# Projections of three tiles in three passes over w_main instead of four, with a weight ring of four chunks

## The chip, the cores and the metric

The kernel runs on one core of one Trainium2 chip. Its engines each run their own instruction stream and wait for each other by semaphores: TensorE (PE, matmuls, with weight loads listed as PEld), VectorE (DVE), ScalarE (ACT), GpSimd (POOL) and SyncE (SP), the last of which only issues DMAs here. The metric is the time of one execution on the device in microseconds; lower is better.

## The reference

One step of a one-layer streaming trunk in float32, for 1040 prompt rows (16 meta rows and 1024) and 32 sample rows that have 1040 cached rows before them. Per row it normalises x, projects it, runs two kinds of attention of 8 heads each, gates and merges them, and adds a product-key mixture: 128 experts per row (8 heads, 16 each) out of 16384, picked as the top 16 of the 256 sums of two top-16 lists.

```python
n = rms_norm(x, norm_mix)
fq, fk, fv, ff, sq, sk, sv, ga, gb = split(n @ w_in)      # 3*512 | 8 | 3*512 | 2*1024 columns
o_fox = fox_attention(fq, c[:, past:], fk_all, fv_all, c, q_pos, k_pos)
o_sb = stick_breaking_attention(sq, sk_all, sv_all, q_pos, k_pos)
y = (sigmoid(ga) * (o_fox @ w_o_fox) + sigmoid(gb) * (o_sb @ w_o_sb)) @ w_out
h = x + y
xt = rms_norm(h, norm_ffn)
act = gelu(einsum('thkd,td->thk', expert_u[eidx], xt))
out = h + einsum('thk,thkd->td', softmax(sc) * act, expert_v[eidx])
```

## The kernel before

The 1072 rows are nine tiles of 128 (tile 8, called SAMPLES, has 32 sample rows and the 16 meta rows). `WAVES` makes five waves of them: tiles 0 and 1, 2 and 3, 4 and 5, 6 and 7, and tile 8. Every wave g passes through project(g), attend(g) and merge(g). All five engines are written out in full by hand, in program order; there is no scheduler, and order between engines is by semaphores alone.

- **project(g)** (PE line 927, ACT 1186, DVE 1534, SP 603). `NEW` names the tiles that are projected in front of wave g: 0, 1 and SAMPLES for wave 0, then two each, and none for wave 4. `w_main` (all of w_in but the forget columns, 1024 x 5120) is read once per project call in ten columns of 512, each in two halves of 512 rows: twenty chunks of 1 MB. A chunk goes into the ring `wring` of `NW` = 3 buffers, which the merge's chunks (`w_stream`, 16 per wave) share. PE multiplies each half column with every tile's turned x (`xt`, for the third tile `xt_s`) into that tile's bank (`column_bank`, six: four of `pb` and two halves of `pv`), ACT copies it out to `stage` and stores it, q and k columns (`QK`) are also turned on PE. Before the first column PE waits for `xg_ready`: DVE multiplies the turned x by norm_mix once x_t is there. `forget()` on PE is the small product for the forget columns.
- **attend(g)**: 32 units (16 in wave 4), each a head, a tile and a kind. The keys and values of a pair of heads are loaded by SP (`load_pair`, line 516), from DRAM where the projection stored them. The first pair of waves 1 to 3 is issued inside project(g), at c == 7.
- **merge(g)**: products with w_o, gates, w_out, the residual, the norm, the expert queries, the picking of experts (`pick_halves`, `pick_experts` on DVE, the last of which raises `named`).
- **Expert work of the tiles of wave g - 1** runs beside the stages of wave g. POOL gathers for each of 128 slots a row of expert_u and expert_v for each of 128 rows (1 MB) into one of ten buffers `uv`. A lot is four slots: DVE makes four dots (line 1346), ACT the gelu, and each slot's sum is made on DVE (line 1369) or on PE (`background`, line 777). `Plan` deals the 64 lots of two tiles over the steps of the wave in proportion to `SHARE`; `ON_VECTOR` says how many of a lot's four sums DVE makes beside a step of that kind: four in projections, y and h, two in most of the merge, none while experts are picked, and in attention three in two lots (the default).

The lots of wave 1, 2 and 3 each: 13 in the projection, 26 in attention, 15 in the merge to the queries, 10 in the picking.

On SP everything is in one queue: an issue that has to wait holds all behind it. The arena (`carve`, lines 320 to 391) is one buffer of SBUF whose parts are used by several stages in turn.

## Time and profile before

| | us |
|---|---|
| median of three runs | 4275.64 |
| lowest, highest | 4275.32, 4285.22 |
| the profiled execution, its own time | 4279.13 |
| span of the profile | 4277.3 |
| TensorE, VectorE, ScalarE, GpSimd busy | 3242.6, 2864.9, 1216.8, 1389.5 |
| moved by DMA | 1388.17 MB, mean 325 GB/s |
| wave 0: projection, attention | 25 to 257, 257 to 377 |
| wave 1: projection, attention, merge | 601 to 832, 832 to 1129, 1129 to 1489 |
| wave 2: the same | 1491 to 1732, 1732 to 2053, 2053 to 2411 |
| wave 3: the same | 2413 to 2656, 2656 to 3028, 3028 to 3380 |
| wave 4: attention, merge; then the rest of the experts | 3395 to 3662, 3662 to 3930; to 4277 |

Busy time is that of one engine's instructions, a sum over stages with different limits. In a view of stretches, a row gives the stretch, its length, then the busy time and the number of instructions of PE, PEld, DVE, ACT and POOL, the granted clock of TensorE as a share of full speed, the busy share of the DMA engines and GB/s. In a timeline a row gives start, length, engine, line, operation, output and inputs by name, count, and in brackets the idle time before it and what ended it.

### The profile page before, as it was taken

How to read it: one execution, taken by the hardware profiler on the slowest of the kernel's cores; microseconds unless marked ns; L12 is line 12 of the kernel's file. 1: busy time of each engine (PE TensorE's matmuls, PEld its weight loads, DVE VectorE, ACT ScalarE, POOL GpSimd, SP SyncE). 2: the span in 40 equal slices, each digit the busy share in tenths (PEclk: the TensorE clock that was granted, in tenths of full speed). 3: DMA queues.
4: the chain of work that ended last, by engine and by line, in shares of the span. 5: the costliest groups of instructions: out<-in, count | busy, mean ns of one | idle time of the engine just before them, and what ended most of it. 6: DMA issues, size and time to landing. Idle time of an engine off the chain costs nothing.

```text
span 4277.3 us, 32195 instructions
## 1 busy us (share of the span) xinstructions
PE 3242.6 (76%) x9738; PEld 1679.2 (39%) x9738; DVE 2864.9 (67%) x5568; ACT 1216.8 (28%) x2591; POOL 1389.5 (32%) x1086
## 2 busy tenths in 40 slices
PE   8989838588868595798876785899876677868665
PEld 3345623244435242455453332555453233334222
DVE  2012477587678975688579775788679766557865
ACT  1132112255311121566111121666211245111110
POOL 0000013243433333343333232334333233434553
PEclk9966969687879798788888897888888777888787
DMA  4413439899999889799999798787998788999997
GB/s 138 134 53 120 141 139 415 335 380 400 391 370 386 322 328 414 279 383 374 390 392 360 278 400 345 298 348 307 384 391 328 277 316 324 408 420 385 385 420 321
DMA packets 306602, 1388.17 MB, mean 325 GB/s; under 512 B 36384, under 2 KB 96960, under 8 KB 159968
## 3 DMA queue, kind: packets, MB, share of 16 engines
q0 software_dynamic: 154464, 1116.02, 64.7%
q1 hardware_dynamic: 121056, 243.75, 15.9%
q10 hardware_dynamic: 30912, 26.35, 1.9%
q8 instruction: 80, 1.31, 0.1%
q14 instruction: 90, 0.74, 0.0%
HBM read 1350.49 MB, written 35.10 MB: 324 GB/s over the span
## 4 chain that ended last, share of the span: by engine, by line
PE 35%; DVE 28%; DMA 18%; ACT 7%; issue 6%; SPq 5%; POOL 1%; ACTq 0%; DVEq 0%; POOLq 0%
DVE uv L1346 11%; PE pb L946 9%; DMA uv<-expert_uv,rows_u 8%; PE pv L777 7%; SPq L526 5%; DMA arena<-w_main 5%; PE pb L887 3%; PE pb L860 3%; PE pb L730 3%; PE pb L759 2%; PE pb L835 2%; DVE held L1369 2%; DMA arena<-w_stream 2%; PE pv L946 2%; DVE arena L1407 1%
## 5 line engine op out<-in xcount | busy, mean ns | idle before, releaser
L680 POOL DMA_INDIRECT uv<-expert_uv,rows_u x1024 | 1334.8, 1304 | 2250.8 <-PE pv L777 1168.8
L777 PE MATMUL pv<-uv,diag 128*128 128x512 f32 x2316 | 1244.7, 694 | 377.4 <-ACT diag L1083 336.9
L1346 DVE CUSTOM_DVE_ANT_0 uv<-uv,nr 128x1024 f32<-128x1024 f32 x1056 | 1241.5, 1220 | 204.8 <-DMA uv<-expert_uv,rows_u 171.0
L777 PEld LDWEIGHTS pv<-uv,diag 128*128 128x128 f32 x2316 | 504.0, 226 | 1024.7 <-issue 982.4
L946 PE MATMUL pb<-arena 128*128 128x512 f32 x1280 | 620.9, 643 | 163.2 <-DMA arena<-w_main 163.1
L1369 DVE SCALAR_TENSOR_TENSOR held<-uv,wgt,held 128x1024 f32<-128x1024 f32 x477 | 613.0, 1285 | 16.9 <-DVE wgt L1357 0.3
L1090 ACT ACTIVATE gel<-dots 128x4 f32<-128x4 f32 x264 | 54.2, 205 | 1792.2 <-DVE dots L1346 1712.5
L946 PEld LDWEIGHTS pb<-arena 128*128 128x128 f32 x1280 | 258.9, 207 | 497.0 <-issue 316.9
L730 PE MATMUL pb<-arena 64*128 64x512 f32 (+6 forms) x544 | 281.2, 635 | 125.2 <-DVE arena L1328 43.0
L759 PE MATMUL pb<-arena 128*128 128x64 f32 (+3 forms) x1728 | 256.2, 297 | 40.3 <-ACT o L1072 40.3
L759 PEld LDWEIGHTS pb<-arena 128*128 128x128 f32 (+3 forms) x1728 | 237.1, 202 | 106.6 <-issue 68.5
L887 PE MATMUL pb<-arena 128*128 128x256 f32 (+1 forms) x1280 | 265.7, 367 | 4.5 <-ACT arena L1156 4.5
L887 PEld LDWEIGHTS pb<-arena 128*128 128x128 f32 x1280 | 230.6, 196 | 46.1 <-issue 12.4
L1357 DVE TENSOR_TENSOR wgt<-gel,gw 128x4 f32<-128x4 f32 x256 | 41.7, 163 | 282.2 <-ACT gel L1090 281.7
L1083 ACT ACTIVATE diag<-ident,wgt 128x128 f32<-128x128 f32 x579 | 194.1, 391 | 85.7 <-PE pv L777 59.3
L1336 DVE SCALAR_TENSOR_TENSOR arena<-arena 128x144 f32<-128x144 f32 (+4 forms) x72 | 59.8, 830 | 211.8 <-ACT arena L1037 207.5
L730 PEld LDWEIGHTS pb<-arena 64*128 64x128 f32 (+1 forms) x544 | 104.1, 223 | 244.6 <-issue 138.6
L701 POOL DMA_DIRECT2D held<-scratch_h x9 | 5.4, 601 | 562.0 <-DVEq L1467 561.7
L747 PE MATMUL pb<-ident,arena 128*128 128x128 f32 (+3 forms) x864 | 144.4, 304 | 44.2 <-ACT arena L1061 43.6
L1090 ACT ACT_TABLE_LOAD x130 | 166.8, 1283 | 7.4 <-ACT arena L1230 5.3
L835 PE MATMUL pb<-arena 128*128 128x512 f32 (+1 forms) x288 | 135.1, 627 | 27.1 <-DMA arena<-w_stream 25.8
L1061 ACT ACTIVATE arena<-pb 128x512 f32<-128x512 f32 (+2 forms) x224 | 94.5, 452 | 191.0 <-PE pb L747 189.0
(147 smaller groups left out, 2670.5 us busy)
## 6 DMA issues: line engine op xcount, KB each, us to landing
arena<-w_main SPq DMA_DIRECT2D x80, 1024.0 KB
arena<-w_stream SPq DMA_DIRECT2D x80, 1024.0 KB
uv<-expert_uv,rows_u POOLq DMA_INDIRECT x1024
arena<-x SPq DMA_DIRECT2D x16, 512.0 KB, 19.6
scratch_gates<-arena ACTq DMA_DIRECT2D x32, 256.0 KB, 11.3
arena<-scratch_gates SPq DMA_DIRECT2D x8, 1024.0 KB, 21.7
arena<-scratch_c_p SPq DMA_DIRECT2D x8, 520.0 KB
arena<-x_t SPq DMA_DIRECT2D x8, 512.0 KB
```

The source lines that it names most:

```text
L526: here = lambda dst, src: sp.dma_start(dst, src).then_inc(pair_in[b], 16)
L680: pool.indirect_dma_start(out=uv[k % NU][:].rearrange("p a n -> p (a n)"), out_offset=None, in_=io["expert_uv"][:, :], in_offset=bass.Indi ...
L730: mm = nc.tensor.matmul(pb[0:r, m % 3, 0:c1 - c0], qt[k][pair % 2][half, tj * P:tj * P + r], kt[k][pair % 2][half, c0:c1], start=True, sto ...
L759: mm = nc.tensor.matmul(po[0:r], probt[n % 2][0:w, slot, 0:r], vt[k][pair % 2][0:w, slot, hh * DH:(hh + 1) * DH], start=j == 0, stop=j == ...
L777: mm = nc.tensor.matmul(pv[:, c * BANK:(c + 1) * BANK], diag[n % ND][:], uv[k % NU][:, 1, c * BANK:(c + 1) * BANK], start=n == first, stop ...
L835: mm = nc.tensor.matmul(pb[0:r, ti * 2 + k, :], ot[:, k * 4 + f, ti * P:ti * P + r], wring[n % NW][:, f * BANK:(f + 1) * BANK], start=f == ...
L887: mm = nc.tensor.matmul(pb[:, 4 + h % 2, half * 2 * P:half * 2 * P + width], wring[n % NW][:, (f * 2 + half) * P:(f * 2 + half + 1) * P], ...
L946: mm = nc.tensor.matmul(column_bank(proj.slot(c, ti))[0:r], x_turned(ti, half * 4 + f, r), w[:, f, :], start=half == 0 and f == 0, stop=ha ...
L1083: nc.scalar.activation(diag[n % ND][:], ident[:], ACT.Copy, scale=wgt[b % 2][:, k % LOT:k % LOT + 1]).then_inc(diag_made, 1)
L1090: nc.scalar.activation(gel[b % 2][:], dots[b % 2][:], ACT.Gelu).then_inc(gelu, 1)
L1346: nc.vector.tensor_tensor_reduce(out=u, in0=u, in1=row[:], scale=1.0, scalar=0.0, op0=ALU.mult, op1=ALU.add, accum_out=dots[b % 2][:, k % ...
L1369: nc.vector.scalar_tensor_tensor(out=held[t % 2][:], in0=v, scalar=w[:, k % LOT:k % LOT + 1], in1=held[t % 2][:], op0=ALU.mult, op1=ALU.ad ...
```

## The change

`NEW` becomes (0, 1, SAMPLES), (2, 3, 4), (5, 6, 7) and nothing in front of waves 3 and 4. Passes over w_main go from four to three, and `NW` from 3 to 4.

- Three tiles take turns over four banks of `pb` (`bank`), in the order of their products, and PE waits until the copy of the product four before is made (`behind`). Slots of `stage` are six, by tile and parity of the column.
- The turned x of the third tile (`xt_third`) lies where picking works; SP loads it behind the first four weight chunks and, in waves 1 and 2, behind a wait for `named`.
- Room for the fourth ring buffer comes from moves in the arena: x of the merge (`xh`) now lies in the output rows `o`, so its load waits for `o_turned`; the picks' buffers, the queries and the row of norm_ffn (`g_row`) lie in the gates, so the load of norm_ffn waits for `merged` and stands in front of the first query chunk.
- `Plan` weighs a projection step by its tiles over two (1.4 becomes 2.1). The lots of waves 1 and 2 become 18 in the projection, 23 in attention, 14 and 9 in the merge; those of wave 3: 32 in attention, 20 in the merge to the queries, 12 in the picking.

```diff
-NW = 3
+NW = 4
-NEW = [(0, 1, SAMPLES), (2, 3), (4, 5), (6, 7), ()]
+NEW = [(0, 1, SAMPLES), (2, 3, 4), (5, 6, 7), (), ()]
...
+    def bank(self, g, c, ti):
+
+        return (c * len(NEW[g]) + ti) % 4
+
+    def behind(self, g, c, ti):
+
+        n = c * len(NEW[g]) + ti - 4
+        return self.staged[g, n // len(NEW[g]), n % len(NEW[g])] if n >= 0 else None
...
-            steps = [(("project", g, c), "project", SHARE["project"]) for c in range(COLS if NEW[g] else 0)]
+            steps = [(("project", g, c), "project", SHARE["project"] * len(NEW[g]) / 2) for c in range(COLS if NEW[g] else 0)]
...
-            count = self.tiles[g][0] * LOTS - first - (0 if NEW[g] else LEFT)
+            count = self.tiles[g][0] * LOTS - first - (0 if g < len(WAVES) - 1 else LEFT)
...
-        o = [[sb(f"o{k}{i}", [P, WID]) for i in range(2)] for k in range(KINDS)]
+        o_rows = [sb(f"o{i}", [P, KINDS, WID]) for i in range(2)]
+        o = [[o_rows[i][:, k, :] for i in range(2)] for k in range(KINDS)]
+        xh = [o_rows[i][:].rearrange("p k n -> p (k n)") for i in range(2)]
...
                     for c in range(NW):
                         load_half(g, c)
+                    if g:
+                        sp.wait_ge(named, plan.tiles[g][0])
+                    t = NEW[g][2]
+                    sp.dma_start(xt_third[:, :, 0:rows_of(t)],
+                                 io["x_t"][:, first_row(t):first_row(t) + rows_of(t)].rearrange("(k p) n -> p k n", p=P)).then_inc(xt_in, 16)
...
+                    sp.wait_ge(o_turned, tiles[-1] + 1)
                     for ti, t in enumerate(tiles):
                         r = query_rows(t)
                         sp.dma_start(xh[ti][0:r], io["x"][first_row(t):first_row(t) + r, :]).then_inc(x_in[ti], 16)
-                    sp.dma_start(g_row, io["norm_ffn"].partition_broadcast(P)).then_inc(g_in, 16)
                     for c in range(NW, 8 + NW):
+                        if c == NW + 4:
+                            sp.wait_ge(merged, 2 * (tiles[-1] + 1))
+                            sp.dma_start(g_row, io["norm_ffn"].partition_broadcast(P)).then_inc(g_in, 16)
                         load_chunk(g, c)
...
-                            if c >= 2 and half == 0:
-                                pe.wait_ge(staged, proj.staged[g, c - 2, ti])
+                            if half == 0 and proj.behind(g, c, ti):
+                                pe.wait_ge(staged, proj.behind(g, c, ti))
...
-                    pe.wait_ge(xg_ready, KD * (g + 1) + 1)
+                    pe.wait_ge(xg_ready, (KD + 1) * (g + 1))
```

Three places in the order of the built programs follow, since the sizes of the ring and of a pass move instructions that the diff doesn't name.

SP, the end of wave 1's projection, before: `w_main` is a weight chunk, `scratch_q_fox` to `out_sv_p` are the first attention pair (its loads of meta rows are left out), `scratch_c_p` the running forget sums.

```order
L561 DMA arena<-w_main 128x4x512 [waits proj_ready]
L526 DMA arena<-scratch_q_fox 128x256 [waits s_stored2,s_stored0,s_stored1,t_stored3,s_stored3,t_stored2,summed_up,t_stored1,t_stored0]
L526 DMA arena<-scratch_k_fox 128x528
L526 DMA arena<-out_fv_p 128x4x128
...
L526 DMA arena<-scratch_k_sb 128x528
L526 DMA arena<-out_sv_p 128x4x128
...
L561 DMA arena<-w_main 128x4x512 [waits chunk_used]
```

The same place after:

```order
L572 DMA arena<-w_main 128x4x512 [waits chunk_used]
L572 DMA arena<-w_main 128x4x512 [waits proj_ready]
L537 DMA arena<-scratch_q_fox 128x256 [waits s_stored1,s_stored3,s_stored4,s_stored0,s_stored2,t_stored3,s_stored5,t_stored2,summed_up,t_stored1,t_stored0]
L537 DMA arena<-scratch_k_fox 128x528
L537 DMA arena<-out_fv_p 128x4x128
```

The twentieth weight chunk stood behind the pair, and now stands ahead of it.

PE, wave 1, from the first chunk to the second of column 1, before: line 946 is a tile's product with a half column, line 962 the turning of a column, `chunk_in` a landed weight chunk, `staged` ACT's copy.

```order
L946 MATMUL pb<-arena 128x512 [waits chunk_in2]
L946 MATMUL pb<-arena 128x512 x7
L962 MATMUL pb<-ident,arena 128x128 [waits col_turned_out,normed]
L962 MATMUL pb<-ident,arena 128x128 x3
L946 MATMUL pb<-arena 128x512 [waits chunk_in0]
```

The same place after, with lines 965 and 981:

```order
L965 MATMUL pb<-arena 128x512 [waits chunk_in2]
L965 MATMUL pb<-arena 128x512 x3
L965 MATMUL pb<-arena 128x512 [waits staged]
L965 MATMUL pb<-arena 128x512 x3
L965 MATMUL pb<-arena 128x512 [waits staged]
L965 MATMUL pb<-arena 128x512 x3
L981 MATMUL pb<-ident,arena 128x128 [waits col_turned_out,normed]
L981 MATMUL pb<-ident,arena 128x128 x3
L965 MATMUL pb<-arena 128x512 [waits chunk_in3]
```

Column 1 waited for no copy before; now its second and third tile wait for the copies of column 0.

SP, from the last merge chunks of wave 2 to wave 3, before:

```order
L553 DMA arena<-w_stream 128x2048 [waits q_ready] x5
L582 DMA arena<-x_t 128x8x128 [waits q_ready,h_stored]
L582 DMA arena<-x_t 128x8x128
L588 DMA arena<-x 128x1024 [waits h_stored]
L588 DMA arena<-x 128x1024
L561 DMA arena<-w_main 128x4x512 [waits q_ready] x3
L561 DMA arena<-w_main 128x4x512 [waits chunk_used]
```

And after:

```order
L564 DMA arena<-w_stream 128x2048 [waits q_ready] x4
L537 DMA arena<-scratch_q_fox 128x256 [waits named,summed_up,q_out,h_stored]
L537 DMA arena<-scratch_k_fox 128x1040
L537 DMA arena<-out_fv_p 128x8x128
L537 DMA arena<-out_fv_p 16x128
L537 DMA arena<-scratch_q_sb 128x256
```

The loads of the projection are gone, and the first pair of wave 3 stands behind the naming of the experts.

## Rows read from the trace of the kernel before

**Rows 1.** The page: busy us by engine, share of the span, instructions.

```profile
PE 3242.6 (76%) x9738; PEld 1679.2 (39%) x9738; DVE 2864.9 (67%) x5568; ACT 1216.8 (28%) x2591; POOL 1389.5 (32%) x1086
```

**Rows 2.** Stretches: length, busy us by engine, clock, DMA share, GB/s; waves 0 to 3.

```profile
25.50:257.00 231.50, 220.98 (x535) 82.86 (x534) 24.25 (x58) 39.03 (x65) 0.00 (x0) 0.99 0.36 113
607.80:832.50 224.70, 163.53 (x359) 71.01 (x358) 142.24 (x207) 43.76 (x67) 69.79 (x50) 0.85 0.86 340
832.50:1129.00 296.50, 249.33 (x824) 133.40 (x824) 240.81 (x384) 170.69 (x365) 134.54 (x106) 0.82 0.95 382
1732.00:2053.00 321.00, 285.27 (x1032) 165.00 (x1032) 266.49 (x392) 200.75 (x412) 134.12 (x106) 0.82 0.91 363
2656.00:3028.00 372.00, 336.05 (x1273) 194.05 (x1274) 294.24 (x403) 230.62 (x429) 137.05 (x106) 0.82 0.84 326
3028.00:3250.00 222.00, 171.03 (x581) 107.57 (x582) 158.96 (x380) 29.53 (x63) 75.32 (x59) 0.87 0.94 378
3250.00:3385.00 135.00, 80.44 (x152) 32.89 (x151) 125.53 (x318) 20.70 (x53) 51.07 (x41) 0.80 0.82 320
```

**Rows 3.** The same view: program start, wave 1's projection, its end.

```profile
24.00:28.00 4.00, 4.00 (x20) 2.58 (x21) 0.00 (x0) 0.00 (x0) 0.00 (x0) 1.00 0.41 142
650.00:700.00 50.00, 43.21 (x106) 19.27 (x104) 43.12 (x62) 15.11 (x26) 23.02 (x16) 0.93 1.03 415
800.00:832.00 32.00, 10.04 (x16) 4.04 (x16) 3.40 (x4) 5.43 (x6) 1.75 (x1) 0.61 0.55 211
```

**Rows 4.** Timeline, TensorE, wave 1's projection: start, us, idle before and its releaser.

```profile
700.65 7.13 PE L946 MATMUL pb<-arena 128*128 128x512 f32 x16 [2.64 <-DMA arena<-w_main]
...
713.15 10.14 PE L946 MATMUL pb<-arena 128*128 128x512 f32 x16 [4.93 <-DMA arena<-w_main]
```

**Rows 5.** Timeline, the end of wave 1's projection: SP's issues and TensorE.

```profile
793.35 0.96 SPq L561 DMA_DIRECT2D arena<-w_main  x1
...
815.76 1.22 PE L946 MATMUL pb<-arena 128*128 128x512 f32 x1 [23.32 <-DMA arena<-w_main]
```

**Rows 6.** Timeline: last naming and next start, wave 3, then wave 4.

```profile
2405.60 1.23 DVE L1346 CUSTOM_DVE_ANT_0 uv<-uv,nr 128x1024 f32<-128x1024 f32 x1 [0.18 <-DVE gw L1464]
...
2656.79 2.07 PE L730 MATMUL pb<-arena 64*128 64x512 f32 x2 [7.87 <-DMA arena<-scratch_c_p]
...
3375.05 0.33 SPq L526 DMA_DIRECT2D arena<-scratch_q_fox  x1
...
3395.19 1.03 PE L730 MATMUL pb<-arena 64*32 64x512 f32 x1 [19.27 <-DMA arena<-scratch_c_s]
```

**Rows 7.** The page: background products, dots, sums (busy, mean ns), gathers, x loads.

```profile
L777 PE MATMUL pv<-uv,diag 128*128 128x512 f32 x2316 | 1244.7, 694 | 377.4 <-ACT diag L1083 336.9
L1346 DVE CUSTOM_DVE_ANT_0 uv<-uv,nr 128x1024 f32<-128x1024 f32 x1056 | 1241.5, 1220 | 204.8 <-DMA uv<-expert_uv,rows_u 171.0
L1369 DVE SCALAR_TENSOR_TENSOR held<-uv,wgt,held 128x1024 f32<-128x1024 f32 x477 | 613.0, 1285 | 16.9 <-DVE wgt L1357 0.3
q0 software_dynamic: 154464, 1116.02, 64.7%
arena<-x SPq DMA_DIRECT2D x16, 512.0 KB, 19.6
```

**Rows 8.** Timeline at the program's start.

```profile
6.67 2.64 SPq L582 DMA_DIRECT2D arena<-x_t  x3
...
14.37 2.19 DVE L1597 TENSOR_SCALAR arena<-arena,g_mix 128x256 f32<-128x256 f32 x8 [10.07 <-DMA arena<-x_t]
...
17.17 8.35 PE L933 MATMUL pb<-wff,arena 128*128 128x8 f32 x48 [17.17 <-DVE arena L1599]
...
25.45 1.22 PE L946 MATMUL pb<-arena 128*128 128x512 f32 x1
```

**Rows 9.** Groups by line within 2413 to 2656, wave 3's projection: ScalarE.

```profile
L1230 ACT ACTIVATE arena<-pb,arena 128x512 f32<-128x512 f32 x20 | 13.6, 687 | 46.1 <-PE pb L946 43.8 <-DMA out_fk_p<-arena 2.0 <-DVE wgt L1357 0.2
L1230 ACT ACT_TABLE_LOAD x4 | 5.1, 1283 | 49.8 <-issue 37.6 <-PE pb L946 12.1
```

More of the change, by code:

```diff
@@ L351, in stream @@
         ot = carve(KD, 2 * P)
-        merged_at = at[0]
         mt = carve(KD, 2 * P)
-        xh = [carve(D) for _ in range(2)]
-        project_end = at[0]
-        g_row = carve(D)
-        qh = [carve(2, 2 * P) for _ in range(2)]
-        rest = [carve(4, NK) for _ in range(2)]
         top = [carve(2, HEADS, TOPK) for _ in range(2)]
@@ L362, in stream @@
         sc, ex, ci = carve(HEADS, TOPK), carve(HEADS, TOPK), carve(HEADS, TOPK).bitcast(U32)
+        g_row = gate[1][:, 1, :]
+        rest = [gate[0][:, 0, i * BANK:(i + 1) * BANK].rearrange("p (j n) -> p j n", j=4) for i in range(2)]
+        qh = [gate[0][:, 1, i * BANK:(i + 1) * BANK].rearrange("p (a q) -> p a q", a=2) for i in range(2)]
+        n2t = ot
+        hit = gate[0].rearrange("p k (h n) -> p (k h) n", h=HEADS // 2).rearrange("p h (a b) -> p h a b", a=TOPK)
+        cand = gate[1].rearrange("p k (h n) -> p (k h) n", h=HEADS // 2)
+        rest2 = mt
+        at[0] = gates_at + KINDS * D
         cab, caf = carve(2, HEADS, TOPK).bitcast(U32), carve(2, HEADS, TOPK)
@@ L371, in stream @@
         sq = carve(BANK)
-        tst_more = [carve(BANK) for _ in range(2)]
+        tst = [carve(BANK) for _ in range(2)]
         ss, rstd = carve(ABREAST), carve(ABREAST)
@@ L475, in x_turned, with cols_to @@
         def x_turned(ti, k, r):
-            return xt[:, k, ti * P:ti * P + r] if ti < 2 else xt_s[:, k, 0:r]
-        def column_bank(slot):
-            return pb[:, slot, :] if slot < 4 else pv[:, (slot - 4) * BANK:(slot - 3) * BANK]
+            return xt[:, k, ti * P:ti * P + r] if ti < 2 else xt_third[:, k, 0:r]
+        def cols_to(g):
+            return sum(COLS for x in NEW[:g] if x)
         def chunk_no(g, c):
-            return g * (2 * COLS + CHUNKS) + c - (0 if NEW[g] else 2 * COLS)
+            return 2 * cols_to(g) + g * CHUNKS + c - (0 if NEW[g] else 2 * COLS)
         def wait_chunk_used(eng, n):
-            g, c = divmod(n, 2 * COLS + CHUNKS)
-            used = g * (COLS + 4)
-            if not NEW[g]:
-                c += 2 * COLS
-                used -= COLS
+            g = max(i for i in range(len(WAVES)) if 2 * cols_to(i) + i * CHUNKS <= n)
+            c = n - chunk_no(g, 0)
+            used = cols_to(g) + g * 4 - (0 if NEW[g] else COLS)
             if c < 2 * COLS:
@@ L1200, in store_column @@
                         for ti, t in enumerate(tiles):
-                            r, sem = rows_of(t), s_stored[proj.slot(c, ti)]
-                            row = stage[proj.slot(c, ti)]
+                            r, sem = rows_of(t), s_stored[proj.slot(g, c, ti)]
+                            row = stage[proj.slot(g, c, ti)]
                             if c == 1:
@@ L1539, in head_norms @@
                             r = rows_of(t)
-                            row = stage[proj.slot(c, ti)][0:r]
+                            row = stage[proj.slot(g, c, ti)][0:r]
                             dve.wait_ge(staged, proj.staged[g, c, ti])
@@ L1597, in project @@
                         nc.vector.tensor_scalar(xt[:, k, :], xt[:, k, :], g_mix[:, k:k + 1], None, ALU.mult).then_inc(xg_ready, 1)
[L1598 to L1599 removed]
+                    third = xt_third[:, :, 0:rows_of(tiles[2])]
+                    nc.vector.tensor_tensor(third, third, g_mix[:].unsqueeze(2).to_broadcast([P, KD, rows_of(tiles[2])]),
+                                            ALU.mult).then_inc(xg_ready, 1)
                     for ti, t in enumerate(tiles):
```

56 lines of the change are left out of this document (25 added, 31 removed).

## The prediction

> **What bounds the kernel now.** I read the page's busy times first: TensorE is busy 76% of the span, VectorE 67%, so no engine bounds the whole [rows 1]. Then the stages, wave by wave [rows 2]. In wave 0 no expert work runs, TensorE is busy 221 of 231.5 us and the DMA engines a third of it: the matmuls bound the projections. In waves 1 to 3 experts run beside everything, and the DMA share is 0.82 to 0.95. Look at the GB/s column: a stretch that is saturated shows 415 GB/s [rows 3], and stages at 380 are close to it, while the projection of wave 1 (340) and the attention of wave 3 (326) are not. The last end differs by stage: in attention of wave 1 the gathers (0.95), in that of wave 3 TensorE (336 of 372 us, 90%), in the picking of experts VectorE (125.5 of 135). A projection loses its time where weights come late: with gathers running, the next half column starts 12.5 us after the one before, though its matmuls take 7 to 10 [rows 4]; and the last half comes 23.3 us late, because SP issues the eight loads of the first attention pair ahead of it and comes to that weight chunk at 793 only [rows 5]. Behind it the DMA rate falls to 211 [rows 3].
>
> So the kernel alternates between limits, and what counts is what each wave's sum does.
>
> **The change, stage by stage.** The sum is made against the profiled execution, 4279.1 us (span 4277.3); it lies 3.5 us above the median 4275.6.
>
> *Removed in wave 3.* The projection goes. Expert naming of wave 2 ends at 2405.6, attention starts at 2656.8 [rows 6]: 251.2 us. In its place stands what wave 4, which never had a projection, shows: SP waits for the naming, then issues the pair and the c row, naming ends at 3375.05 and TensorE starts at 3395.2 [rows 6], 20.1 us. The pair is of like size (keys and values of about 1040 rows). Saved 251.2 - 20.1 = 231.
>
> *Moved into wave 3's other stages.* Its projection carried 13 lots of four slots. They don't vanish: attention goes from 26 lots to 32 (every step has one now), the merge to the queries from 15 to 20, picking from 10 to 12. Attention: 6 lots are 15 slots on TensorE, each 1244.7/579 = 2.15 us [rows 7], 32 us, at the 90% at which TensorE runs there 36. VectorE gets 24 dots at 1.22 and 9 sums at 1.29 [rows 7], 41 us on 294, below TensorE's 368. Gathers are 1116/1056 = 1.06 MB each [rows 7], 25 MB; with the stage's own 121 MB that is 147/415 = 353 us, also below. I take +40; bounds 20 (waits absorb it) and 78 (25.4 MB at the stage's 326). Merge to the queries: it runs at 378 GB/s, so the bytes set it: 21 MB at 415 are 51 us, VectorE's 159 grows by about 41 to 200 of 222 and stays below. I take +48, bounds 30 and 56 (at 378). Picking is VectorE's: 8 dots more, +10. Sum +98, so wave 3: -231 + 98 = -133.
>
> *Waves 1 and 2, projections.* Each has three tiles instead of two and 18 lots instead of 13. Two floors. TensorE: wave 0 has as many projection matmuls, its tensor work is 221 us at a granted clock of 0.99 [rows 2], the forget matmuls before it take 8.35 [rows 8], and the third tile's wider turns and a background lot come in: 240. DMA: today's 340 x 224.7 = 76 MB, 20 gathers more (21 MB), a third tile's rows and stores (3.5 MB): 101 MB, at 415 243 us. The two floors now lie on each other (today 164 and 184). Weights: at the 12.5 us a chunk of today's saturated stretch [rows 4], against 10.6 us of matmuls in a half column (3/2 of the 7.13 of [rows 4]), some 2 us are lost per half, 40 in all; the ring of four can't make bytes, but with it all twenty halves are issued ahead of the pair, so the last 23.3 us wait goes. I take 270 from the first column to attention, against 224.7 today, and 3.5 for the third tile's forget matmuls: +49; wave 2 +48. Bounds 243 and 297 (101 MB at today's 340).
>
> *Waves 1 and 2, the rest.* Five lots leave: three from attention, two from the merge. Attention of wave 1: 12.7 MB at 382 are 33 us, the engines' share about 15; -26. Wave 2, nearer to TensorE's limit (285 of 321): -20. Merge: -15 each (8.5 MB at 378 would be 22, its VectorE part 10).
>
> *The third tile's x, turned.* It lies where the picks lie, so its load waits for the last naming, and SP has it behind the weights; who waits is VectorE (the multiply by norm_mix), behind that the first matmul. Wave 1 has no lot to cover it: the load's landing (at the program's start the x_t loads, issued by 9.3, could be used at 14.4 [rows 8]) and a multiply of 1024 columns, 1.2 us, come in: +6. Wave 2: a lot of 5 us covers part, but gathers compete; loads of this size (x) land after 19.6 us in the median [rows 7], so between 3 and 16: +8. Wave 0: third x_t now stands behind four weight chunks on the queue. Three chunks and the rest, 5.4 MB, had landed by about 26 us (between 24 and 28 the DMA engines are busy 0.41), 0.31 MB per us from 8.5 on; one chunk more and the short tile give about 30, then multiply and forget 11, so the first column starts at 41 instead of 25.45 [rows 3, 8]: +15.
>
> In that: a load issued first is worked on first. VectorE had its x_t at 14.4 while weights landed until 26 [rows 3, 8]. The Trainium skill (DMA: Bandwidth & Descriptors, Queues, rings and completion order) says that each DMA engine takes descriptors in ring order, but that a later one may finish before an earlier; were that to let the third tile through, the +15 would be 0 and the sum 15 lower. The trace shows no such overtaking, but has no case of a small load behind large ones.
>
> *At nothing.* x and norm_ffn are loaded later in the merge: x after the outputs are turned, with the products with w_o and the first with w_out still to come before it is added; norm_ffn after the merged rows, with the whole product with w_out and its lots over it. If a landing of 30 us is not covered, up to 5 us in each of five merges. Four w_stream chunks ahead instead of three may give that back. Banks: four instead of six, see the second rival. Dot and sum split: 470 sums instead of 477.
>
> Sum: wave 0 +15; wave 1 +6 +49 -26 -15 = +14; wave 2 +8 +48 -20 -15 = +21; wave 3 -133. Together -83: 4279 - 83 = 4196 profiled, 4193 in the median.
>
> **Cross-check by bytes.** Twenty chunks less, 21 MB, are 51 us at 415 GB/s. The other 32 us must come from a better filled wave 3: its attention moves 121 MB, 292 us of the 372 at full rate. Plausible, not certain.
>
> **Rivals.**
> First, *the moved lots cost the full pace*. If each of the 13 lots costs in wave 3 what a lot's share of the stage is today (372/26 = 14.3 us in attention, 357/25 = 14.3 in the merge) they cost 186 and not 98: 4193 + 88 = 4281, no change that a run could tell. For it: stages scale by latency chains, not by busy time. Against: six attention steps have no lot today and VectorE or TensorE idle in them. 0.07.
>
> Second, *the lead of one column, slower*. Today a column's matmuls wait for ScalarE to have taken the column two before; now, with four banks, the second and third tile wait for the column just done. ScalarE takes it only after the gelus of the step before, which wait for VectorE's dots: up to a lot, 4 x 1.22 + 4 x 1.29 = 10 us, or 7 (dots, a table load 1.28, a copy 0.69 [rows 9]) once per column. Twenty columns at 7 are +140: 4333. It outweighs the gain from 83/20 = 4.1 us per column. Against: today ScalarE waits 43.8 us for TensorE in wave 3's projection [rows 9], so it is early, and turning and the first tile lie between. For: the third tile's stores are issued on ScalarE too, and it has been held by issuing for 37.6 us once [rows 9]. 0.09.
>
> Third, *weights never late, faster*. Larger halves and a ring of four could hide every chunk, and both projections fall to their floor: 27 us less each, and the attention behind them finds its pair and c row in place, for which it waits 7.87 us today in wave 3 [rows 6], 8 each: 4193 - 70 = 4123. As a mechanism here: if the weights' queue had half of 415 beside the gathers', 1.05 MB would take 5 us, well under 10.6. The Trainium skill (DMA: Bandwidth & Descriptors, Queues, rings and completion order) says so in effect: a DMA engine goes round robin between its queues, a packet each. [rows 4] speak against it: one chunk per 12.5 us is 84 GB/s. 0.12.
>
> Fourth, *not what it says*: that weights are loaded as often. The built program has 60 loads of w_main where it had 80, so I give it 0.02.
>
> **Chances.** My forecast 0.70, its own span 4150 to 4250 (attention and merge of wave 3 at their bounds -38 or +46, projections -25 to +25 each). A measurement of this kernel can tell about 0.3%, 13 us, from no change. Faster: 0.70 + 0.12 and a little of the first rival's edge, 0.83; same 0.07; slower 0.10. The range takes in most of the third rival and the upper bounds: 4135 to 4262.
>
> **What would show it.** w_main issues 60. Wave 0's first column at about 41 us; waves 1 and 2 with 270 us of columns, TensorE's wait for w_main some 40 each and none of 23 at the end; no wait of ScalarE's copies (staged) above 10 us in sum. Wave 3's attention starts 20 us after naming and takes 412, its merge 270 + 145. DMA mean rate up from 325. The forecast is wrong if a three-tile projection takes over 320, or wave 3's attention over 450.

## The result and the profile after

The changed kernel takes 4223.2 us in the median (4222.2 to 4228.0), the kernel before beside it 4275.5: a ratio of 0.9877, 95% interval 0.9858 to 0.9897. That is 52 us faster; 83 were forecast. The profiled execution has a span of 4221.9 us against 4277.3, so the traces differ by 55.4.

The page after, busy times, then the projection's matmuls (after the bar: idle time ahead of them and who ended it), then DMA issues (KB each, us to landing):

```profile
PE 3201.1 (76%) x9766; PEld 1661.7 (39%) x9766; DVE 2854.8 (68%) x5552; ACT 1198.4 (28%) x2584; POOL 1367.6 (32%) x1086
...
L965 PE MATMUL pb<-arena 128*128 128x512 f32 (+1 forms) x1440 | 651.9, 611 | 35.5 <-ACT arena L1249 35.5
...
arena<-w_main SPq DMA_DIRECT2D x60, 1024.0 KB, 9.5
```

The shares are those of [rows 1], since busy time fell with the span: TensorE's by 41.5 us, and 39.6 of them lie in the same 1280 matmuls of the projection, before and then after:

```profile
L946 PE MATMUL pb<-arena 128*128 128x512 f32 x1280 | 620.9, 643 | 163.2 <-DMA arena<-w_main 163.1
```

```profile
L965 PE MATMUL pb<-arena 128*128 128x512 f32 x1280 | 581.3, 613 | 35.5 <-ACT arena L1249 35.5
```

One takes 613 ns where it took 643, at a granted clock of 0.93 in wave 1's columns against 0.85 before. So a part of the gain in the columns is TensorE's clock; no run here holds the clock fixed to tell the two apart. These matmuls no longer wait for weights at all (163 us in the trace of before), but 35.5 us for ScalarE's copies. The loads are 60. To see where 55 us come from, the span must be cut at the same events. These marks are read off the timelines (first and last matmul of a stage; "named" is VectorE's last instruction of naming):

| us, before -> after | wave 1 | wave 2 | wave 3 |
|---|---|---|---|
| naming to first column | 9.3 -> 17.7 | 14.5 -> 26.2 | 14.5 -> none |
| columns | 217.9 -> 259.9 | 226.6 -> 272.6 | 229.0 -> none |
| last column to first score matmul | 6.7 -> 29.1 | 7.4 -> 35.3 | (naming to attention) 251.4 -> 18.3 |
| attention | 296.6 -> 272.7 | 320.9 -> 312.3 | 371.1 -> 398.3 |
| merge and picking | 354.8 -> 332.9 | 352.2 -> 329.5 | 347.0 -> 402.6 |
| whole wave | 885.3 -> 912.3 | 921.5 -> 975.9 | 969.5 -> 819.2 |

Wave 0 goes from 598.6 to 614.6 us, wave 4 with the rest from 902.4 to 899.9. So +16.0 + 27.0 + 54.4 - 150.3 - 2.5 = -55.4.

The stretches after, in the columns of [rows 2]: wave 1's columns, the gap behind them, attention and merge of wave 1, then of wave 3 the attention, the merge to the queries, and picking:

```profile
632.30:892.20 259.90, 226.44 (x535) 101.43 (x535) 181.44 (x266) 49.67 (x84) 88.89 (x63) 0.93 0.86 333
...
892.00:921.00 29.00, 0.19 (x1) 0.00 (x0) 19.20 (x26) 6.10 (x8) 12.73 (x10) 0.57 1.02 415
921.00:1194.00 273.00, 235.51 (x796) 127.48 (x796) 218.76 (x352) 160.34 (x349) 110.80 (x91) 0.81 0.96 378
1194.00:1527.00 333.00, 244.46 (x715) 137.34 (x716) 266.24 (x668) 47.20 (x108) 112.47 (x91) 0.85 0.93 370
2521.00:2919.00 398.00, 356.15 (x1352) 198.91 (x1352) 333.55 (x465) 253.11 (x465) 164.34 (x132) 0.88 0.93 366
2919.00:3180.00 261.00, 178.68 (x596) 109.77 (x595) 195.70 (x430) 31.83 (x71) 96.37 (x76) 0.85 0.96 390
3180.00:3322.00 142.00, 97.16 (x187) 39.86 (x187) 136.97 (x337) 23.08 (x64) 64.89 (x51) 0.86 0.91 364
```

Against [rows 2]: wave 3's attention went from 326 to 366 GB/s and to 0.93 of the DMA engines, its VectorE from 294 to 334 us busy, TensorE from 336 to 356. The empty room was filled.

In wave 1's columns TensorE is idle for 33.5 us. Who ended that idle time (us in all, times, longest):

```profile
PE pb L965 <- ACT arena L1249: 16.5, 3, 12.3
PE pb L981 <- ACT arena L1213: 10.6, 5, 5.2
PE pb L981 <- ACT o L1213: 6.3, 2, 4.8
```

All three are ScalarE's copies: of a column (L1249), for which the products wait, and of a turned column (L1213), for which the turning waits. They are the whole idle time of the columns; in wave 2 they are 40.3 us of 40.3. Before, such waits were 4.6 us in wave 1's columns and 2.3 in wave 2's.

Behind the columns stands the second line of the stretches: 29 us in which TensorE does nothing while the DMA engines run at their full 415 GB/s. The timeline of the end of wave 1's projection, ScalarE and its queue, SyncE's queue, then TensorE (in brackets: idle before, and what ended it); TensorE's last column ends at 892.2:

```profile
870.01 14.57 SPq L537 DMA_DIRECT2D arena<-out_sv_p  x2
...
897.36 0.20 ACT L1109 ACTIVATE gel<-dots 128x4 f32<-128x4 f32 x1 [11.58 <-DVE dots L1365]
897.58 1.28 ACT L1249 ACT_TABLE_LOAD   x1
898.87 1.27 ACT L1249 ACTIVATE arena<-pb,arena 128x512 f32<-128x512 f32 x2
899.59 0.33 ACTq L1231 DMA_DIRECT2D scratch_gates<-arena  x1
...
913.77 0.80 SPq L558 DMA_DIRECT2D arena<-scratch_c_p  x2
...
921.32 1.70 PE L749 MATMUL pb<-arena 64*128 64x400 f32 x2 [29.12 <-DMA arena<-scratch_c_p]
```

Read it from the bottom. TensorE waits for the row of the gates' sums (`c_p`), which SyncE asks for at 913.8, once everything that the projection stores has landed. The last of that are the gates, stored at 899.6, since ScalarE copies the last column only behind a gelu that waits for VectorE's dots until 897.4. And SyncE issued the first pair's values only at 870. The forecast had no term for this: it ended the stage at the last weight.

### The profile page after: what moved, and what is told of

Its sections match the earlier page's. It is cut to its first block, busy times and chain, and to the rows that moved or that the text cites. A ratio compares the mean times of both kernels' runs of the same rounds, so it can differ in the third digit from the quotient of the medians.

```text
span 4221.9 us, 32194 instructions
## 1 busy us (share of the span) xinstructions
PE 3201.1 (76%) x9766; PEld 1661.7 (39%) x9766; DVE 2854.8 (68%) x5552; ACT 1198.4 (28%) x2584; POOL 1367.6 (32%) x1086
## 4 chain that ended last, share of the span: by engine, by line
DVE 22%; DMA 12%; PE 11%; ACT 5%; issue 5%; SPq 2%; POOL 1%; ACTq 0%; DVEq 0%; POOLq 0%
DVE uv L1365 10%; DMA uv<-expert_uv,rows_u 8%; PE pv L796 5%; DVE held L1388 2%; SPq L537 2%; DVE arena L1356 1%; PE pb L906 1%; DMA uv<-expert_uv,rows_pk 1%; DMA arena<-scratch_gates 1%; POOL uv L699 1%; PE pb L854 1%; PE pb L749 1%; ACT L1140 1%; PE pb L879 1%; DVE arena L1426 1%
## 5 line engine op out<-in xcount | busy, mean ns | idle before, releaser
L699 POOL DMA_INDIRECT uv<-expert_uv,rows_u x1024 | 1311.7, 1281 | 2203.1 <-PE pv L796 1225.8
L796 PE MATMUL pv<-uv,diag 128*128 128x512 f32 x2344 | 1263.8, 696 | 404.2 <-ACT diag L1102 329.5
L965 PE MATMUL pb<-arena 128*128 128x512 f32 (+1 forms) x1440 | 651.9, 611 | 35.5 <-ACT arena L1249 35.5
L1388 DVE SCALAR_TENSOR_TENSOR held<-uv,wgt,held 128x1024 f32<-128x1024 f32 x470 | 603.9, 1285 | 16.6 <-DVE wgt L1376 0.3
L965 PEld LDWEIGHTS pb<-arena 128*128 128x128 f32 (+1 forms) x1440 | 266.6, 189 | 398.4 <-issue 357.5
L906 PEld LDWEIGHTS pb<-arena 128*128 128x128 f32 x1280 | 228.4, 195 | 42.1 <-issue 12.9
L1347 DVE SCALAR_TENSOR_TENSOR arena<-arena,cq,pb 128x512 f32<-128x512 f32 (+5 forms) x136 | 70.9, 557 | 148.0 <-PE pb L753 86.5
```

The source lines that it names most:

```text
L699: pool.indirect_dma_start(out=uv[k % NU][:].rearrange("p a n -> p (a n)"), out_offset=None, in_=io["expert_uv"][:, :], in_offset=bass.Indi ...
L796: mm = nc.tensor.matmul(pv[:, c * BANK:(c + 1) * BANK], diag[n % ND][:], uv[k % NU][:, 1, c * BANK:(c + 1) * BANK], start=n == first, stop ...
L906: mm = nc.tensor.matmul(pb[:, 4 + h % 2, half * 2 * P:half * 2 * P + width], wring[n % NW][:, (f * 2 + half) * P:(f * 2 + half + 1) * P], ...
L965: mm = nc.tensor.matmul(pb[0:r, proj.bank(g, c, ti), :], x_turned(ti, half * 4 + f, r), w[:, f, :], start=half == 0 and f == 0, stop=half ...
L1388: nc.vector.scalar_tensor_tensor(out=held[t % 2][:], in0=v, scalar=w[:, k % LOT:k % LOT + 1], in1=held[t % 2][:], op0=ALU.mult, op1=ALU.ad ...
```

## The experiments

All ratios are to the kernel before, run beside; one us of difference between kernels is 0.00023. "Gap" is the time from TensorE's last column to its first score matmul.

**The ring of four and the moved loads, with four passes as before.** `NEW` goes back to two tiles a wave; NW = 4 and the rest of the change stay.

```diff
-NEW = [(0, 1, SAMPLES), (2, 3, 4), (5, 6, 7), (), ()]
+NEW = [(0, 1, SAMPLES), (2, 3), (4, 5), (6, 7), ()]
...
```

> The changed kernel with the tiles of the kernel before: three tiles in wave 0 and two in front of each of waves 1, 2 and 3, four passes over w_main (80 loads); ring of four chunks, moves in the arena and order of the loads as changed. It separates the ring and the moves from the passes. Theory A (the gain is the pass saved; the ring only moves the wait at the end of a projection from the last weight chunk, 23 us, to the c row behind the pair's loads): wave 0 costs its +15, the rest is even, 4275 + 15 = about 4290 (4275 to 4300). Theory B (the ring of four alone takes away the waits for w_main, 50 us a wave): 4275 + 15 - 3 x 45 = about 4155. TensorE's idle time before w_main: A has some 50 to 90 us of it left, B next to none, and both show it in the profile.

4250.0 us, ratio 0.9934 (0.9910 to 0.9958), 28 us below before and between the two expectations. The columns take 184, 201 and 200 us, against 218, 226 and 229 before; the gap goes from 7 to 29.2, 25.8 and 28.2. TensorE's waits in this kernel (us in all, times, longest), then in the kernel before:

```profile
PE pb L964 <- DMA arena<-w_main: 86.5, 16, 12.5
PE pb L748 <- DMA arena<-scratch_c_p: 94.2, 4, 29.2
```

```profile
PE pb L946 <- DMA arena<-w_main: 163.1, 25, 23.8
```

The 23 us at the last weight [rows 5] did not go away; they moved behind the column. Before, the pair's eight loads were issued in front of the last half, so the weight was late and the pair was there. Now the weight is there and the pair is late. What stays of 33, 26 and 29 us in the columns is 11, 7 and 9 us a wave. That is the first theory's mechanism, the wait moved, with a gain that it did not have; of the second theory's 45 us a wave it leaves a fifth. Here too a part is the clock: in wave 1's columns the waits for w_main fall from 49.7 to 25.2 us, and TensorE's busy time from 163.5 to 154.5 at a clock of 0.91 for 0.85.

**Three passes with a ring of three.**

```diff
-NW = 4
+NW = 3
...
-                        if c == NW + 4:
+                        if c == 8:
```

> The changed kernel with the weight ring back at three chunks; everything else as changed, three passes. Theory A (ring size does nothing for the sum: the last chunk stands behind the pair again and TensorE waits some 23 us for it, but VectorE's lots and the c row end the stage as before): 4223 +- 12. Theory B (each projection ends with both waits, the weight chunk's and the c row's): 2 x 23 more, about 4269.

4262.6 us, ratio 0.9958 (0.9944 to 0.9972). The columns take 306 and 318 us, the gap 7.6 and 7.7; TensorE waits 89.9 us for w_main in five waits, the longest 36.8. So the same trade shows from the other side: columns and gap of wave 1 take 313 us with three chunks, 289 with four. The time is near the second theory's 4269, but its reason, both waits at once, is not there: the wait for the row is back to 8 us, and the one for weights is longer than the 23 that both theories had. The ring alone brings 28 us, the passes alone 18, both 52; without the loss in wave 0 that each of them has (14.9, 12.4 and 16.0) 43, 30 and 69: the two parts nearly add.

**The third tile's rows asked for first in wave 0.**

```diff
                     if g:
                         sp.wait_ge(q_ready, wave_heads(g))
+                    else:
+                        load_third(g)
...
                     if g:
                         sp.wait_ge(named, plan.tiles[g][0])
...
+                        load_third(g)
```

> The changed kernel with one load moved: in wave 0 the third tile's turned x is loaded in front of everything else of that wave instead of behind four weight chunks. My sum priced this place at +15 and the trace shows the first column 14.7 us later. If wave 0 is bound by its matmuls from there, all of it comes back: first column at about 26 us, time 4223 - 15 = 4208. If the later waves take it up (gathers start at a naming that moves with it, so they can't): 4223.

4209.0 us, ratio 0.9837 (0.9812 to 0.9861), against 0.9877. SyncE's issues at the start and the first column in the changed kernel, then the first column here:

```profile
10.54 5.35 SPq L572 DMA_DIRECT2D arena<-w_main  x4
15.93 2.95 SPq L628 DMA_DIRECT2D arena<-x_t  x1
...
40.12 5.49 PE L965 MATMUL pb<-arena 128*128 128x512 f32 x6
```

```profile
25.50 1.22 PE L970 MATMUL pb<-arena 128*128 128x512 f32 x1
```

The first column starts at 25.5 us here and at 40.1 in the changed kernel, and naming in wave 0 ends at 598.4 against 614.6. The term of 15 us is shown whole: it was the place in the queue.

**The row of sums asked for first.** At the end of the projection SyncE asks for the pair's first row before it waits for the last stores; the engines that reuse the stage's memory wait for the stores themselves.

```diff
                     sp.wait_ge(proj_ready, proj.all_staged[g])
+                    if g:
+                        sp.wait_ge(c_stored, 16 * (g + 2))
+                        sp.wait_ge(s_stored[0], proj.all_s[g][0])
+                        load_ck(2 * plan.first_pair[g])
...
+                        if g:
+                            stores_done(dve, g)
```

> The changed kernel; in waves 1 and 2 SP issues the first c row as soon as the projection's chunks, sums and the one overlapping store are done, and no longer behind all stores of the gates; TensorE waits for ScalarE's last copies instead, VectorE and ScalarE for the stores. Today TensorE waits 29.1 and 35.3 us there for the row. Theory A (the row's load is the cause): TensorE starts attention some 20 us earlier in each wave and all follow, 4223 - 40 to 50 = about 4178. Theory B (VectorE is behind by its lots and ScalarE with it; TensorE's idle time there costs little): VectorE ends its last lot about 6 us before the row is in, so 5 to 8 us a wave, about 4210.

4214.7 us, ratio 0.9860 (0.9832 to 0.9887). TensorE in this kernel:

```profile
879.57 12.18 PE L978 MATMUL pb<-arena 128*128 128x512 f32 x28
916.17 1.67 PE L762 MATMUL pb<-arena 64*128 64x400 f32 x2 [24.42 <-DMA arena<-scratch_c_p]
```

The row is asked for at 891.8 in place of 913.8, and TensorE starts 5 us earlier; in wave 2 the gap stays at 35.4. The number fits the second theory, though its interval overlaps the changed kernel's (0.9858 to 0.9897), and its reason isn't shown by it: TensorE is still released by a DMA, 24 us after the row was asked for. The trace shows what stands in the queue ahead of it: the last piece of the pair's values, asked for at 873.4, lands 39.4 us later, at 912.8, and the row 3 us behind it, at 916.0.

**Thirteen lots in a projection instead of 18.**

```diff
-            steps = [(("project", g, c), "project", SHARE["project"] * len(NEW[g]) / 2) for c in range(COLS if NEW[g] else 0)]
+            steps = [(("project", g, c), "project", SHARE["project"]) for c in range(COLS if NEW[g] else 0)]
```

> The changed kernel with one factor taken out of the lots' plan: a projection step of three tiles has the same weight as one of two tiles had, so 13 lots stand in each of the two later projections in place of 18; the 5 others go to the attention (26 for 23) and the merge (25 for 23). Nothing else moves. Theory A (after TensorE's last column the stage waits for VectorE, which still has lots queued, and ScalarE's last copy, the stores of the gates and the row of gates stand behind them): the gap from TensorE's last column to its first score matmul falls from 29.1 and 35.3 us to 8 to 15, and the columns themselves (259.9 and 272.7) get shorter by 5 to 20, since ScalarE waits less for VectorE; but attention and merge take the lots back at some 12 us a lot, where the engine has no more room than before: the whole within 10 us of 4223. Theory B (the gap is the stores and the row's transfer under the gathers' load, whatever VectorE does): the gap stays above 25 us, the columns stay, attention and merge grow by 20 to 25 us a wave, and the time is 4255 to 4270.

4211.9 us, ratio 0.9834 (0.9818 to 0.9850): 18 us better than the changed kernel by the ratios, 12 by the spans. The columns get shorter by more than either theory had, to 230.4 and 241.9 us (from 259.9 and 272.6):

```profile
630.10:860.50 230.40, 217.09 (x535) 97.75 (x535) 145.25 (x221) 52.94 (x83) 67.37 (x48) 0.97 0.84 321
860.50:883.10 22.60, 0.03 (x2) 0.02 (x1) 5.30 (x5) 3.46 (x4) 4.83 (x4) 0.55 1.03 406
```

Of the 29.5 us in wave 1's columns 20 are waits for ScalarE's copies, which fall from 33.4 to 13.3, and 9 are TensorE's busy time (226.4 to 217.1), at a clock of 0.97 for 0.93. So the lots did hold the columns. That they do it by way of the gelus, which stand ahead of the copies in ScalarE's program, is likely and not tested by itself. Attention takes the lots back with 25 and 8 us, the merge with 15 and 17. The gaps are 22.6 and 24.1 us, between the theories (8 to 15, above 25). VectorE is idle through most of the gap (busy 5.3 of 22.6 us) and yet most of the gap is there: VectorE's queue, theory A's reason, can have made the 6.5 and 11.2 us that went, and not the rest. Theory B's columns and total are wrong too. In wave 1 a lot costs 6 us in the columns and 8 elsewhere, in wave 2 6 and 5, so what is gained lies in wave 2 (959.2 against 975.9), while wave 1 loses 4.

**Logarithms grouped.** First the three exponentials, then the three logarithms: two table loads for six.

```diff
+                        for ti, t in enumerate(tiles):
+                            r = rows_of(t)
                             nc.scalar.activation(ffa[0:r, ti], ffa[0:r, ti], ACT.Ln, bias=1.0).then_inc(ff_log, 1)
```

> The changed kernel, ScalarE's logarithms of the forget gates grouped: first the three exponentials, then the three logarithms, so two activation tables are loaded in place of six in each projection (1.28 us each, 5.1 us less for each of three waves on ScalarE). Theory A (ScalarE's burst after the third column is what lets TensorE's copies and VectorE's weights run late): the wait of VectorE for the gelu of 21.4 us and that of TensorE for the copy of 12.3 us in wave 1 get shorter by about 5 us each, and the time falls by 5 to 12 us to some 4211 to 4218. Theory B (the burst is made up for before the column's end, because VectorE's lots end the stage): the columns' end moves by less than 2 us, time 4219 to 4225.

4214.8 us, ratio 0.9843 (0.9827 to 0.9859), span 4207.0. ScalarE in the changed kernel:

```profile
723.87 1.28 ACT L1262 ACT_TABLE_LOAD   x1 [15.89 <-issue]
725.17 0.21 ACT L1262 ACTIVATE arena<-arena 128x8 f32<-128x8 f32 x1
725.40 1.28 ACT L1263 ACT_TABLE_LOAD   x1
726.69 0.21 ACT L1263 ACTIVATE arena<-arena 128x8 f32<-128x8 f32 x1
```

The columns take 254.5 and 267.8 us, 5.4 and 4.9 less: the four table loads of 1.28 us each, as theory A had it. The rest of the 15 us between the spans lies in small pieces over five waves and is not explained.

**The three edits together**, third rows first, row first, logarithms grouped.

> The changed kernel with the three small edits together: the third tile's rows loaded first in wave 0, the first row of the gates' sums asked for before the rest of the stage's end, and the logarithms grouped. If they are independent their gains add: 14.2 (measured alone) + 8.6 (measured alone) + what the grouped logarithms give alone (0 to 12): 4190 to 4201. If the second and the third work on the same wait (VectorE's lots behind the last column), the sum is 5 to 8 us short of that: 4198 to 4205.

4198.4 us, ratio 0.9804 (0.9788 to 0.9820). The time lies in both expectations (4190 to 4201 and 4198 to 4205) and decides nothing between them. By the ratios the three gains would add up to 0.9786 (0.9877 less 0.0040, 0.0017 and 0.0034), 8 us more than came, which intervals of 0.0016 to either side don't set apart from noise. The gaps are 24.6 and 35.4 us.

**The same with no lot in the last column.** Weight 0.3 in place of 2.1 for the last step.

> As the combined kernel, but the last column of a projection has no lot (weight 0.3 in place of 2.1), so 17 lots stand in a projection and the one goes to the attention (24 for 23). If VectorE's queue at the last column is what the stage's end waits for, one lot less just there takes 8 to 12 us off the gap and gives 10 to 12 us back in the attention: within 4 us of the combined kernel. If only the order at the end matters (the last lot in front of the last copy on ScalarE), the gap falls and nothing comes back: 8 to 15 us faster than the combined kernel.

4206.1 us, ratio 0.9823 (0.9806 to 0.9839). The gaps are 24.5 and 35.7 us, unchanged to 0.3; in attention and merge together wave 1 takes 6 us more and wave 2 3. Neither expectation: the lot in the last column was not in the way, so VectorE's queue there doesn't make the gap.

**The last column first on ScalarE, and the row on its queue.** ScalarE waits for TensorE's last column ahead of the last gelu of the ninth step, asks for the row on its own queue, copies and stores.

```diff
+                    def last_column():
+                        act.wait_ge(proj_ready, proj.all_staged[g])
...
+                        act.dma_start(ck[i % 3][:, 0:w], dram["c_p"][0:1, 0:w].to_broadcast([P, w])).then_inc(ck_in[i % 3], 16)
+                        for ti in range(len(tiles)):
+                            take_column(COLS - 1, ti)
+                        store_column(COLS - 1)
```

> The combined kernel, with the end of the two later projections rearranged on ScalarE: in front of the second gelu of the ninth column's step it waits for TensorE's last column, asks for the row of the gates' sums on its own DMA queue (on SyncE's the row was asked for at 872.6 us, landed 24.5 us later, behind the first pair's keys and values), copies the last column and stores it. Theory A (the gap is the row's place in SyncE's queue and the copies' place behind a gelu): the row lands 8 to 12 us after the last column (the gates' stores on that queue took 7.4 to 8.7 us), the gap falls from 24.6 and 35 us to 10 to 14, each wave gains 10 to 20 us, the lots being done beside the attention; time 4160 to 4180. Theory B (VectorE's queued lots and the transfers' pace under the gathers set the attention's start or its pace): TensorE starts earlier and waits in the attention for VectorE; the gain is under 8 us in all, 4188 to 4200.

4187.6 us, ratio 0.9788 (0.9771 to 0.9804), an interval that overlaps the combined kernel's, at the edge of theory B's 4188 to 4200. The row now lands 8.0 us after it is asked for, as theory A had it, and the gap, for which A had 10 to 14 us, is still 21.7 and 35.0 us. But the releaser has changed:

```profile
849.71 14.98 SPq L545 DMA_DIRECT2D arena<-out_sv_p  x2
...
893.20 1.67 PE L763 MATMUL pb<-arena 64*128 64x400 f32 x2 [21.69 <-DMA arena<-out_sv_p]
```

This is what stood ahead in SyncE's queue: the first pair's values, issued from 849.7 on and used at 893.2. In the changed kernel the last of them landed 39.4 us after 872.8, at 912.2: 20 of the 29 us of its gap were the pair's, and the row, asked for late, made the other 9.

**The same with thirteen lots**, and, to take the two apart, **the combined kernel with thirteen lots** and the old end.

> The same with 13 lots in a projection in place of 18, as in the run with flat lots, which gained some 12 us against the changed kernel by itself (most of it in wave 2, whose columns took 31 us less against 8.5 and 16.5 us more in attention and merge). If the lots' place is worth the same here, it is 8 to 15 us faster than the run before it (4150 to 4170). If that gain was the same wait that the rearranged end takes away (the lots queued behind the last column), the two kernels are within 5 us.

> The combined kernel with 13 lots in a projection in place of 18, the end of the projection as it was there (row of the gates' sums on SyncE's queue, last column copied behind the gelu). In the fastest kernel so far the gap between TensorE's last column and the first score matmul is 3.9 and 4.2 us; there ScalarE waits 20 us for the last column, VectorE's lots and with them the gathers pause, and the DMA rate falls from 415 GB/s to nearly nothing. Theory A (the pause lets the first pair's loads and the row land): without it the gap stays at 15 to 24 us in each wave, and the time is 4180 to 4192. Theory B (fewer lots alone clear the way, and the rearranged end adds nothing to it): the gap is 4 to 10 us and the time 4163 to 4172.

With the rearranged end 4166.5 us, ratio 0.9739 (0.9723 to 0.9755), the best kernel of all and 57 us below the changed one; gaps 3.9 and 4.2 us. With the old end 4186.4 us, ratio 0.9781 (0.9761 to 0.9800); gaps 23.1 and 23.9. The lots are the same, so theory A holds: fewer lots alone don't close the gap. The ends of wave 1's projection, ten us a row, the kernel with the rearranged end first:

```profile
820.00:830.00 10.00, 10.00 (x25) 4.45 (x24) 3.07 (x6) 0.69 (x1) 1.59 (x1) 1.00 1.02 415
830.00:840.00 10.00, 10.00 (x25) 4.48 (x24) 0.00 (x0) 0.00 (x0) 0.00 (x0) 1.00 0.97 362
840.00:850.00 10.00, 6.15 (x10) 1.71 (x8) 4.76 (x5) 3.33 (x5) 2.84 (x2) 0.70 0.45 137
```

```profile
830.00:840.00 10.00, 10.00 (x25) 4.44 (x24) 3.60 (x8) 2.66 (x3) 1.98 (x1) 1.00 1.03 418
840.00:850.00 10.00, 0.95 (x3) 0.12 (x1) 5.30 (x5) 2.18 (x3) 3.71 (x3) 0.70 1.02 409
850.00:860.00 10.00, 0.00 (x0) 0.00 (x0) 0.00 (x0) 1.28 (x1) 1.12 (x2) 0.50 1.04 408
```

TensorE has finished its last column at 841 in both. In the first, ScalarE stands waiting for that column, so no gelu comes, VectorE and the gathers stop under TensorE's last matmuls, and the queue of the gathers runs dry. What SyncE's queue moves from 825 to 840 us (packets, MB, share of the DMA engines), in the kernel with the rearranged end and then with the old one:

```profile
q1 hardware_dynamic: 1752, 1.46, 30.3%
```

```profile
q1 hardware_dynamic: 669, 0.69, 13.0%
```

The DMA issues in 800 to 836 and in 800 to 838 us (KB each, us to landing) give what that does for the pair's last values:

```profile
arena<-out_sv_p SPq DMA_DIRECT2D x1, 256.0 KB, 17.0
```

```profile
arena<-out_sv_p SPq DMA_DIRECT2D x1, 256.0 KB, 30.8
```

The two runs differ in the pause and in the row's queue as well, and no run has the one without the other; the trace tells them apart. With the old end the pair's last piece (8 KB) lands 37.8 us after 825.8, at 863.6, and TensorE starts at 864.1: a row on another queue could have saved it half a us. With the rearranged end the same piece lands 14.9 us after 826.1, at 841.0, and TensorE waits only for the row, 3.6 us after it was asked for instead of the 8.0 in the run before. (In that run, with 18 lots, the same edit makes no pause: 404 to 420 GB/s in every ten us from 840 to 900.) The pause is partly paid for: attention takes 307.4 and 333.6 us against 296.0 and 321.8. Over wave 1 the rearranged end gives 910.0 - 902.6 = 7 us, over wave 2 958.0 - 944.7 = 13.

## Why the prediction was right, and where it was off

The forecast said 4193 (4135 to 4262) with a chance of 0.83 for faster; it came to 4223. Against its steps:

- **Wave 0, +15.** Measured +16.0, and shown by its own experiment. The first column starts at 40.1 (forecast 41). A small load behind large ones waited for them; nothing let it through.
- **Up to the first column of waves 1 and 2, +9.5 and +11.5** (the third tile's x and its forget matmuls): +8.4 and +11.7.
- **The projections, +45 without those matmuls: wrong in size.** Measured from first column to attention +64.4 and +74.0 (to 289 and 308 us, by 270). The columns alone take 260 and 273 us, 17 to 33 above the two floors of 243 and 240: the DMA engines are at 0.86 in them, TensorE is busy 226 of 260. The bytes were forecast well (101 MB; 333 GB/s in the columns and 415 in the gap make 99). The term that failed is the ring's: "all twenty halves are issued ahead of the pair, so the last 23.3 us wait goes". It became a gap of 29 and 35 us at full DMA rate. The forecast asked what else is late only for weights, not for the pair that now goes last. 308 is even outside the bound of 297.
- **"Some 2 us are lost per half", a wait for w_main of 40 us each: wrong.** TensorE waits for no weight. It waits 33 and 40 us for ScalarE's copies instead, so that the columns came near 270 by luck: one cost was taken for another of the same size. The third rival's mechanism, weights never late, came true and its gain of 70 us didn't, since the pair and the row were not "in place" but later than before. With 13 lots the columns are 226 and 238 us with the old end and 226 and 235 with the rearranged one, so what held the columns was the lots, and what the pause shortens is the gap.
- **Lots that leave waves 1 and 2:** attention -23.9 (forecast -26) and -8.6 (-20), merge and picking -21.9 and -22.7 (-15 each). Together -77 against -76, by luck: attention gave less and the merge more.
- **Wave 3.** Naming to attention 18.3 us (20.1). Attention +27.2 instead of +40: VectorE got its 39 us (41 forecast), but TensorE only 20 instead of 32. Its granted clock is 0.88 there against 0.82, which can be why; not tested. Merge and picking +55.6 (58). In sum -150 by -133.
- **The first rival**, moved lots at the full pace: they cost 83 us, not 186, and the forecast had 98.
- **The second rival**, copies that wait behind gelus, is there in part: TensorE waits for ScalarE's copies 33 and 40 us in the two projections, once 15.8 us, against 5 and 2 before. The forecast's "above 10 us" is passed, the rival's 140 us are far. The forecast put this at nothing, "see the second rival", since ScalarE had been early (43.8 us of waiting); with 18 lots and a third tile it no longer is, and with 13 lots the waits in wave 1 are 13 us.
- **Not seen:** the DMA mean rate, forecast up from 325, is 324. Less time, but also 21 MB less.

The sum: -55 by -83, 28 us off. The projections were 19 and 30 us worse than forecast, 49 in all, the size of the two new gaps (22 and 28); wave 3 gave back 17, wave 4 and the small terms the rest. So the direction and the accounting by stages were right, and the total lies in the range partly because the two errors have opposite signs.

## What to carry to other kernels

When a deeper ring lets weights be issued earlier, write down what is now last in that queue, and who waits for it: the wait moves there. Beside the stream of gathers at full rate the first pair's keys and values landed 31 to 44 us after they were asked for, so they have to be asked for that far ahead; where they could not be, a short pause of the gathers while TensorE still had work cost less here than TensorE's wait. Ask too which copies a stage's matmuls wait for, and what stands ahead of them on the copying engine. And a stage that is moved should be costed by the room where it lands: here six lots of a dropped pass went into an attention at 326 GB/s for 27 us.

## What the runs showed of the hardware

In these traces the queues share the DMA engines by count and not by bytes. The queues' packets, MB and share of the engines' time in the kernel before, 690 to 750 us, at 415 GB/s (gathers, SyncE's, ScalarE's):

```profile
q0 software_dynamic: 2296, 16.71, 66.3%
q1 hardware_dynamic: 2863, 5.70, 24.5%
q10 hardware_dynamic: 2891, 2.48, 12.0%
```

Three queues with work move nearly as many packets each, but the gathers' are 7.3 KB and the weights' 2.0 KB: 5.70 MB in 60 us are 95 GB/s, a chunk in 11 us, near the 12.5 of [rows 4]. The same in the kernel with 13 lots and the old end, 820 to 836 us, where SyncE's packets are 1.5 KB:

```profile
q0 software_dynamic: 665, 4.90, 73.1%
q1 hardware_dynamic: 660, 1.01, 16.8%
q10 hardware_dynamic: 432, 0.79, 12.8%
```

The Trainium skill (DMA: Bandwidth & Descriptors, Queues, rings and completion order) says that a DMA engine takes turns between its queues a packet at a time. The traces agree, if the profile's packets are the page's, which no run here shows. They show where the third rival's arithmetic went wrong: it gave the weights half of the bytes.

A DMA issue can hold its engine. In the changed kernel ScalarE's three stores at 709.4 us held it for 11.1 us, and SyncE's two loads of values at 870.0 took 14.6 us to issue; its two loads of the row at 913.8, with the DMA engines just as full but the queue's own loads landed, took 0.8. What makes the issue wait is open. So is what makes wave 2's gap 4 to 13 us longer than wave 1's in the kernels with 17 or 18 lots, three passes and a ring of four; with a ring of three it is the same.
